# Float32 expert queries from raw blocks loaded ahead, and FFN gate and up in 512- and 256-column products

## What is computed

```python
def swiglu(x, w_in, w_out):                 # D_FF = 2816, four of these
    gate, up = jnp.split(x @ w_in, 2, axis=-1)
    return (jax.nn.silu(gate) * up) @ w_out
```

## Time and profile before

| | |
|---|---|
| median of three executions | 2783.86 us |
| the profiled execution, its own time | 2783.54 us |
| its span, first to last instruction | 2781.7 us |
| TensorE matmul busy | 2475.3 us (89%) |
| VectorE, ScalarE, GpSimd busy | 1787.2, 1207.2, 918.7 us |
| mean granted clock of TensorE | 0.963 |
| gathers of experts | 512, 536.90 MB |
| loads by SP and ScalarE | 237.44 MB |
| chain that ended last, largest shares | TensorE 50%, DMA 23% (all of it the experts' gathers) |

### The profile page before, as it was taken

The page is one execution under the profiler, slowest core; times in us unless marked ns, Lnnn a source line. Parts: engine busy times, 40 slices in busy tenths (PEclk is TensorE's granted clock), DMA queues, the critical chain, the costliest instruction groups (busy, mean ns, idle before and its releaser), DMA issues.

```text
span 2781.7 us, 35690 instructions
## 1 busy us (share of the span) xinstructions
PE 2475.3 (89%) x12144; PEld 1762.6 (63%) x12144; DVE 1787.2 (64%) x3702; ACT 1207.2 (43%) x2618; POOL 918.7 (33%) x726
## 2 busy tenths in 40 slices
PE   8999999999899999998888777869888888777788
PEld 8988799999779988986444333324765444333244
DVE  6662566766666665656666767665576676676665
ACT  4446744444574456564333322333463333223324
POOL 0005400000230026665443433443444444433442
PEclk9999999999999999999999999899999999999999
DMA  6554355555435544448999999999339999999996
GB/s 214 186 173 134 129 190 188 182 182 187 140 99 188 190 147 138 143 137 340 414 416 416 419 420 418 416 415 389 129 128 420 409 417 418 420 419 417 412 415 254
DMA packets 141959, 783.52 MB, mean 282 GB/s; under 512 B 15872, under 2 KB 16384, under 8 KB 76288
## 3 DMA queue, kind: packets, MB, share of 16 engines
q0 software_dynamic: 73728, 536.90, 46.6%
q1 hardware_dynamic: 65360, 237.44, 25.2%
q10 hardware_dynamic: 2736, 7.46, 0.9%
HBM read 780.69 MB, written 1.05 MB: 281 GB/s over the span
## 4 chain that ended last, share of the span: by engine, by line
PE 50%; DMA 23%; ACT 8%; issue 7%; POOL 6%; DVE 6%; POOLq 0%; ACTq 0%; SPq 0%; DVEq 0%
DMA arena<-experts,arena 23%; PE ps L633 12%; PE ps L634 12%; PE ps L635 12%; PE ps L1222 6%; PE ps L1225 5%; POOL ring_lo L369 4%; DVE arena L2633 2%; POOL arena L2753 2%; ACT row L1831 2%; ACT arena L1824 1%; ACT L1822 1%; ACT ring_hi L363 1%; PE ps L1116 1%; ACT hT_hi L1441 0%
## 5 line engine op out<-in xcount | busy, mean ns | idle before, releaser
L2633 DVE SCALAR_TENSOR_TENSOR arena<-arena,ps 128x1024 f32<-128x1024 f32 x512 | 618.7, 1221 | 410.0 <-DMA arena<-experts,arena 400.4
L1222 PE MATMUL ps<-arena,row 128*128 128x512 f32 x1024 | 573.4, 643 | 228.7 <-ACT row L1831 216.6
L2753 POOL DMA_INDIRECT arena<-experts,arena x512 | 488.2, 954 | 679.0 <-PE ps L1225 465.6
L633 PE MATMUL ps<-hT_hi,ring_hi 128*128 128x256 f32 (+1 forms) x2024 | 580.6, 287 | 7.8 <-DVE hT_lo L2167 4.0
L634 PE MATMUL ps<-hT_lo,ring_hi 128*128 128x256 f32 (+1 forms) x2024 | 573.6, 283 | 0.0
L635 PE MATMUL ps<-hT_hi,ring_lo 128*128 128x256 f32 (+1 forms) x2024 | 573.5, 283 | 0.0
L363 ACT ACTIVATE ring_hi<-ring 128x1024 fp32r<-128x1024 f32 x436 | 458.4, 1057 | 237.6 <-PE ps L635 234.3
L1225 PE MATMUL ps<-arena,row 128*128 128x512 f32 x1024 | 554.9, 624 | 0.0
L1222 PEld LDWEIGHTS ps<-arena,row 128*128 128x128 f32 x1024 | 197.3, 202 | 509.7 <-ACT row L1831 287.9
L369 POOL TENSOR_TENSOR ring_lo<-ring,ring_hi 128x1024 fp32r<-128x1024 f32 x159 | 382.2, 2412 | 344.3 <-ACT ring_hi L363 264.7
L633 PEld LDWEIGHTS ps<-hT_hi,ring_hi 128*128 128x128 f32 (+1 forms) x2024 | 388.5, 192 | 13.8 <-issue 6.7
(11 more groups left out here) (341 smaller groups left out, 2998.8 us busy)
## 6 DMA issues: line engine op xcount, KB each, us to landing
ring<-stream SPq DMA_DIRECT2D x440, 512.0 KB, 4.4
arena<-experts,arena POOLq DMA_INDIRECT x512
row<-rows_in ACTq DMA_DIRECT2D x11, 512.0 KB, 4.2
arena<-stream SPq DMA_DIRECT2D x8, 512.0 KB, 3.5
x<-x_in SPq DMA_DIRECT2D x1, 1024.0 KB, 4.9
out<-arena SPq DMA_DIRECT2D x2, 512.0 KB, 2.6
arena<-cols_in ACTq DMA_DIRECT2D x3, 256.0 KB, 7.2
cols<-cols_in SPq DMA_DIRECT2D x1, 425.5 KB, 5.6
```

The costliest lines, as they stand in the source:

```text
L633: pe.matmul(dst, a[0], b[0], start=start, stop=False)
L1222: lower = pe.matmul(ps[:, 2 * tb, :], diag, v[:, 0:HALF], start=first, stop=end)
L2633: last = dve.scalar_tensor_tensor(u, u, 1.0, h, ALU.mult, ALU.mult, accum_out=R["a"][:, n % 2, k:k + 1])
L2753: pool.indirect_dma_start(R["held"][:, g % HELD, :], None, experts, bass.IndirectOffsetOnAxis(ap=idx[:, n % 2, k:k + 1], axis=0))\
```

## The change

In the FFN the high and low parts of h become one tile, `hT`, with the parts one after the other. For a gate or up block and each k, the high part of the weights is multiplied by both parts of h at once, 512 columns into a whole PSUM bank, and the low part of the weights by the high part of h, 256 columns into the first half of the bank. VectorE adds the two halves of the bank with a reduction before it scales. The gate's sum and scaling stand one low part earlier in VectorE's order than before.

In the expert layers the query blocks are no longer split. Both they and h are used as float32 in one product per k. All 16 blocks of a layer have a place of their own: 0 and 1 in the arena, 2 and 3 in `w`, 4 to 7 in `ring`, 8 to 11 in `ring_hi`, 12 to 15 in `ring_lo`. Blocks 0 to 3 are loaded before the first block of `ssm_out` or `swa_out`, 4 to 7 as the last low parts of the out projection are ready, 8 to 15 as its last blocks are used. The high and low parts of queries and their h, the unread products and the POOL's low parts between gathers are gone, and with them the hold on gathers 9 to 16. The first queries stand one step earlier in the out projection. The next layer's blocks are loaded to the ring when query blocks 4 to 7 have been used, and their high parts wait for all queries. The rotary angles move from `ffn0` to `stick_breaking`, on VectorE and ScalarE.

```diff
+        hT = sb("hT", [P, 2, KD, T], F32R)
+        hT_hi, hT_lo = hT[:, 0], hT[:, 1]
...
+        later_queries = (plain("queries_in_w", w_at, 2, BLK), plain("queries_in_ring_hi", ring_hi_at, SLOTS, BLK),
+                         plain("queries_in_ring_lo", ring_lo_at, SLOTS, BLK))
+        h_for_queries = plain("h_for_queries", hT_at, KD, T)
...
# SP
+                if b in OUTS:
+                    first_query = AT[f"peer{OUTS[b]}_q"]
+                    if OUTS[b] == 0:
+                        sp.wait_ge(used, AT["ssm_z"])
+                    else:
+                        sp.wait_ge(of("swa_kv"), 1)
+                    for m in range(SLOTS):
+                        sp.dma_start(raw(first_query + m), stream[first_query + m]).then_inc(raw_loaded(first_query + m), 16)
+                if b in QUERY:
+                    l, m = QUERY[b]
+                    if m < SLOTS:
+                        b += 1
+                        continue
+                    if m < 2 * SLOTS:
+                        who, own = SPLIT[b - 2 * SLOTS][1:]
+                        sp.wait_ge(lo_ready[who], own + 1)
+                    else:
+                        sp.wait_ge(used, AT[f"peer{l}_q"] - SLOTS + m % SLOTS + 1)
...
+                if b in NEXT_IN_RING:
+                    sp.wait_ge(used, NEXT_IN_RING[b] + 1)
# TensorE
+                    if k % 2 == 0:
+                        pe.wait_ge(of("peer_hT0_a"), KD * l + k + 2)
+                    last = pe.matmul(ps[:, 0, 0:T], parts_for_queries(k, slice(0, P)), both[:, :, k * P:(k + 1) * P],
+                                     start=k == 0, stop=k == KD - 1)
...
-                elif (half, step) == (0, TAIL - 1):
+                elif (half, step) == (0, TAIL - 2):
                     first_queries(l)
...
+            def split_column_pair(b, bank_at, i=None, per_turn=0, entering=None):
+
+                wait_split(pe, b, i, per_turn)
+                for k in range(KD):
+                    if entering is not None:
+                        wait_hT(entering, k)
+                    hi, lo = ring_parts(b, slice(k * P, (k + 1) * P))
+                    pe.matmul(ps[:, bank_at, :], hi, hT[:, :, k, :], start=k == 0, stop=False)
+                    last = pe.matmul(ps[:, bank_at, 0:T], lo, hT_hi[:, k, :], start=False, stop=k == KD - 1)
+                last.then_inc(used, 1)
...
-                    split_column_block(b, ps[:, 4 + 2 * (c % 2), 0:T], i, 12, v if c == 0 else None)
-                    split_column_block(b + 1, ps[:, 5 + 2 * (c % 2), 0:T], i, 12)
+                    split_column_pair(b, 4 + 2 * (c % 2), i, 12, v if c == 0 else None)
+                    split_column_pair(b + 1, 5 + 2 * (c % 2), i, 12)
...
+                def block_product(m, k, t):
+                    return pe.matmul(query_in(m)[:, t], raw(base + m)[:, k * P:(k + 1) * P], parts_for_queries(k, t),
+                                     start=k == 0, stop=k == KD - 1)
...
-                unread_products(12, 3)
# VectorE, FFN
+                def gate(c, i=None):
+                    dve.wait_ge(used, count(gate_block_of(base, c) + 1, i, 12))
+                    dve.tensor_reduce(sums[:, 0, :].unsqueeze(2), both_halves(4 + 2 * (c % 2)), AX.X, ALU.add)\
+                       .then_inc(of("gate_summed"), 1)
+                    dve.wait_ge(of("gate_summed"), count(done + c + 1, i, 4))
+                    dve.tensor_tensor(hid[:, 2, c % 2, :], sums[:, 0, :], norm_row(), ALU.mult).then_inc(of("gate_scaled"), 1)
...
-                    dve.tensor_tensor(up, ps[:, 5 + 2 * (c % 2), 0:T], norm_row(), ALU.mult).then_inc(of("up_scaled"), 1)
+                    dve.tensor_reduce(sums[:, 1, :].unsqueeze(2), both_halves(5 + 2 * (c % 2)), AX.X, ALU.add)\
+                       .then_inc(of("up_summed"), 1)
+                    dve.wait_ge(of("up_summed"), count(done + c + 1, i, 4))
+                    dve.tensor_tensor(up, sums[:, 1, :], norm_row(), ALU.mult).then_inc(of("up_scaled"), 1)
...
-                        for b in range(3 * c, 3 * c + 3):
-                            make_lo(dve, base + b, i, 12)
+                        make_lo(dve, base + 3 * c, i, 12)
+                        make_lo(dve, base + 3 * c + 1, i, 12)
+                        gate(c, i)
+                        make_lo(dve, base + 3 * c + 2, i, 12)
                         dve.wait_ge(used, i * 12 + (base + 3 * c - 1))
                         hidden(c, i)
...
# POOL, expert layer
-                for m in range(FRONT, FRONT + 2):
-                    make_lo(pool, base + m)
                 pool.wait_ge(of("peer_idx"), UNITS * l + 1)
-                gather(0, range(8, SPARE_PICK))
-                for m in range(FRONT + 2, FRONT + RING):
-                    make_lo(pool, base + m)
-                pool.wait_ge(lo_ready["pool"], SPLIT[base + FRONT + RING - 1][2] + 1)
-                gather(0, range(SPARE_PICK, TOPK))
+                gather(0, range(8, TOPK))
```

More of the change, by code:

```diff
@@ L346, in count, with parts_for_queries @@
             return v if i is None else i * per_turn + v
[L348 to L355, removed]
+        def parts_for_queries(k, t):
+            return h_for_queries[:, k, t]
         def make_hi(act, b, i=None, per_turn=0):
             wait_loaded(act, b, i, per_turn)
[L360 to L363, removed]
+            if b in NEXT_IN_RING:
+                act.wait_ge(used, AT["ple0_proj" if b < AT["peer1_q"] else "ple1_proj"])
+            elif b >= SLOTS:
+                act.wait_ge(used, count(b - SLOTS + 1, i, per_turn))
+            act.activation(ring_hi[:, b % SLOTS, :], raw(b), ACT.Copy).then_inc(hi_ready, 1)
         def make_lo(e, b, i=None, per_turn=0):
@@ L380, in build_program @@
             hT_by[v_ + 1] = hT_by[v_] + KD
+        lows_by = {v: n - KD * sum(v > NORM_OF[f"peer{l}"] for l in range(2)) for v, n in hT_by.items()}
         def bank(k, n=1):
@@ L500, in _ @@
                 end = b
-                while end < n_blocks and end not in SPARE and SPLIT.get(end - RING, (0, "used"))[1] == way and (end == b or end not in HELD_BACK):
+                while end < n_blocks and end not in QUERY and (end == b or end not in OUTS) and SPLIT.get(end - RING, (0, "used"))[1] == way and (end == b or end not in HELD_BACK):
                     end += 1
@@ L623, in wait_hT @@
             def wait_hT(v, k):
-                pe.wait_ge(hT_d, hT_by[v] + (k + 1 if v in [NORM_OF[n] for n in TURNED_APART] else max(k + 1, 2)))
+                pe.wait_ge(hT_d, lows_by[v] + (k + 1 if v in [NORM_OF[n] for n in TURNED_APART] else max(k + 1, 2)))
             def parts_of(v):
@@ L1202, in query @@
                         pe.wait_ge(of("peer_qT"), n0 + m - 1)
-                    split_column_block(base + m, query_in(m))
+                    wait_loaded(pe, base + m)
+                    for k in range(KD):
+                        last = block_product(m, k, slice(0, T))
+                    last.then_inc(used, 1)
                 def key_scores(m):
```

141 lines of the change are left out of this document (58 added, 83 removed).

## The result

The changed kernel takes 2765.89 us (median of four executions, 2765.79 to 2766.08) against 2783.48 us before on the same chip: a ratio of 0.9938, 95% interval 0.9923 to 0.9953. It is faster by 17.6 us (0.6%), as forecast in sign, but by half of the 34 us, and 0.9 us outside the range. The profiled execution has 2766.08 us and a span of 2764.3 us.

A forecast was written before the change was run, and what follows sets the result against it. The prediction took matmul spacing on TensorE to bound the FFNs and DMA bytes the expert stages. FFN -18 and experts -16 make -34 us, from 2783.86 to 2750 us, with a range of 2741 to 2765.

The forecast's parts named there:

- FFN gate and up: TensorE in the FFNs: a 512 plus a 256 product takes 0.347 us for 0.360, 1408 times, 18.7 us off.
- The rival with the pair at 0.355: FFN products: alternation pays the switch each time, 0.355 us per pair; FFN -7, experts -16, 2761 us; chance 0.12.
- FFN ends: VectorE's last low part runs within some 0.3 us of TensorE's need; 0.5 us per FFN as bound, 0.7 for four.
- Bytes: Expert stages: four query blocks of 0.524 MB fewer in the byte-bound stretch, 5.0 us per layer at 419 GB/s.
- Start of the saturated stretch: Expert layer front: eight query blocks issued without VectorE waits fill the windows to 1280 us, 2.0 us per layer.
- The low parts' dips: Query part of expert stages: POOL's low parts ahead of gathers lower the DMA rate; 1.5 us per layer taken.
- The angles: Moving them to stick-breaking costs nothing, under 19.13 us of VectorE idle time; without that cover some 3 us.
- the bad bounds of the FFN term: FFNs: a gain of only 7 us if pairs take 0.355 us; separately, VectorE stalls of 0.5 us per FFN.
- the rival on VectorE: VectorE bounds the FFNs: reading PSUM halves at quarter rate, 2.25 us each, chunk 10.1 us; 2908 us; chance 0.03.
- the one on a change without effect: Early loads find their places taken and the FFN's switch eats the rest: within 0.2%, 2782 us; chance 0.02.
- A saved instruction is worth only some 2 ns: FFN products: fewer instructions save little; FFN -3, experts -16, 2765 us; chance 0.08.
- the expert stages give nothing: Expert stages bound by the chain of picks, later by slots TensorE frees; FFN -18, experts 0, 2766 us; chance 0.12.

The follow-up runs named there:

- run 2: Changed kernel, but each gate or up block does all eight 512-column products first, then all eight of 256 columns: 2762.54 us, ratio 0.9921.
- run 1: Changed kernel with FFN gate and up as before (three 256-column products, no reductions), queries and angles staying changed: 2771.51 us, ratio 0.9958.
- run 7: Changed kernel without the loads of query blocks 12 to 15 in either expert layer, so results differ from the reference: 2755.16 us, ratio 0.9900.
- Run 6: Changed kernel, but VectorE computes the next unit's expert indices before the third group of dot products, not behind it: 2764.61 us, ratio 0.9934.
- runs 1 to 4: Edits of the changed kernel: run 1; run 2; block 63's low part in each FFN on GpSimd (2770.16 us); that together with run 2 (2765.04 us).
- run 5: Changed kernel, but each FFN's last chunk has gate and up as before, without VectorE's two reductions: 2763.15 us, ratio 0.9926.

## Why the prediction was wrong

**FFN gate and up.** The step that failed first is "the mix of forms does not occur before, only the switch between them ... together 0.34 to 0.35, as in the sum": I took one switch from rows and assumed that it repeats. Repeated without a pause it costs 0.3525 us. With three products of 256 at 0.3594 (5.75 us over 16) a pair saves 0.0069 us and not 0.0133: 9.7 us in place of 18.7. The rival with the pair at 0.355 was the nearer one (0.12). The value of a saved instruction was right: with the order changed, run 2 shows 0.3475.

**FFN ends.** The next step that failed is "0.5 us per FFN as a bound, 0.7 us for all four taken": 1.02 us each, 4.1 in all. I had found the place, the last low part, but judged it with a margin of 0.3 us from one chunk's balance, which has a down product in it. In the last chunks there is none, and the backlog adds up. Together 9.7 - 4.1 = 5.6 us, which is what run 1 and the stages show. That VectorE keeps up inside the chunks was right, at 0.69 us a reduction.

**Bytes.** Right: "four blocks less are 5.0 us per layer"; run 7 takes four more away and gets 5.4 of time per layer.

**Start of the saturated stretch.** Right within 0.2 us: from 5 us before the first gather to 20 behind it 9.75 MB move for 9.00, 1.8 us for a forecast of 2.0 (second layer 9.73 for 8.88, 2.0 us). The first gather itself comes 12.2 us behind the layer's transposes for 11.6: the +0.6 us of the longer first queries, in both layers.

**The low parts' dips.** Right in itself (1.3 us for 1.5). But 5.0, 2.0 and 1.5 do not add up to 8.5 us from the first gather to the last: 6.3 and 6.1 us are measured. The step that failed is that I took the stage as limited by bytes at every moment, so that a lead once won is kept. Behind the queries the rate fell (414 for 418 GB/s from 250 us on), while GpSimd waited 208.5 us for indices in all, for 153.2 before. Run 6 took that wait away, and the layers did not end sooner: what it won ahead was lost in the last 25 us, at slots that TensorE frees. So the layer sits close to other limits, and which of them keeps the missing 2.2 to 2.5 us is open. A layer came out 5.1 to 5.7 us shorter, and not 7.9. Over the changed kernel and runs 1 to 4, whose expert layers are the same, a layer takes 637.5 to 640.3 us, 639.2 on average, for 645.4: 6.1 us less, so part of what is missing lies within what varies from kernel to kernel.

**The angles.** "Costs nothing" was right, "some 3 us" without cover was wrong by far: the operations lasted 17.7 us (below) and used up the 19 us of cover. VectorE no longer idles before it scales the values, and does so 30.2 us behind the stage's start for 28.4; the stage is no longer for it.

**The sum.** By run 1, -5.6 for the FFNs and -12 for the experts, the measured -17.6. Against the forecast of -34 the FFN term misses 12 us and the expert term 4. The range did not hold it because the bad bounds of the FFN term (-7, and stalls of 0.5 us each) were set one at a time; both happened, the stalls twice as large. Taken together as recorded they give -5, and with the experts' -9 a range to 2770. Of the signs named, the first FFN is 1.7 us shorter for 4 to 5, and its chunk is above 8.35 us though TensorE does not wait for VectorE in it. The chance of 0.95 for "faster" leaves out the rival on VectorE (0.03) and the one on a change without effect (0.02), not the last two of the list.

Two rivals name almost the measured time, and by luck. "A saved instruction is worth only some 2 ns" (2765) is out by run 2, where it is worth 12 to 13 ns, and "the expert stages give nothing" (2766) by run 1, where they give 12 us.

## What to carry to other kernels

A spacing taken from one switch in a trace does not price a loop that switches at every instruction: where products of two sizes can be sorted by kind, or by twos, sort them. An engine's margin must be added up over the stretch in which the other engine's filler work is missing (the end of a pipeline), not over a steady period. In a stage bound by bytes, bytes taken away paid in full here, but a lead won by filling gaps did not last to the end of the stage: look at what issues its last transfers before you count the lead as time.

## What was new of the hardware

- Products of 512 and 256 columns of this type in strict alternation take 0.3525 us a pair; sorted in eights or in twos 0.3475 (5.56 us for 16 pairs).
- Small VectorE operations beside GpSimd's low parts wait for them. The angles before the change, in the first FFN with GpSimd idle, and after it, in stick-breaking beside seven low parts:

```profile
28.83 0.64 DVE L2296 TENSOR_SCALAR arena<-cols,posf 128x16 f32<-128x16 f32 x4
29.51 0.19 DVE L2299 TENSOR_SCALAR arena<-arena 128x48 f32<-128x48 f32 x1
```

```profile
215.61 9.39 DVE L2334 TENSOR_SCALAR arena<-cols,posf 128x16 f32<-128x16 f32 x4
225.03 2.34 DVE L2337 TENSOR_SCALAR arena<-arena 128x48 f32<-128x48 f32 x1
```

```profile
213.14 16.53 POOL L381 TENSOR_TENSOR ring_lo<-ring,ring_hi 128x1024 fp32r<-128x1024 f32 x7
```

  0.19 us becomes 2.34, GpSimd's 2.36 us a piece: VectorE gets one operation in between two of GpSimd's. Eight operations with one input in PSUM were free of it: from 204.58 on, beside a piece of GpSimd's from 204.32 to 206.70, eight low parts of h from PSUM take 3.23 us, 0.40 each.
- TensorE's granted clock falls to its lower level for some 3 us in stages with gaps; in stick-breaking this cost 1.6 us. It fell behind 3.25 and 3.24 us of work in 5 us in two kernels (before, run 5) and did not behind 3.24 in the changed one.
